# A hybrid backbone step: denser front, spread loads, early root and bias, context attention inside the Hyena stage

## What is computed

```
sh1,sc1,g1,sh2,sc2,g2 = silu(cond) @ w_mod + b_mod       # 1024 x 6144, two cond vectors
u   = layer_norm(x) * (1 + sc1) + sh1
q,k,v,xr,gate,hy = u @ w_in                              # 1024 x 2816
att = softmax(q k / 8 [+ rel. position bias]) v          # context: 128 x 128 keys, 8 heads of 64
                                                         # latent: window of the grid + 128 cached keys
rg  = bidirectional RG-LRU(xr) * gelu(gate)              # scans over tokens; has a sqrt
hyo = order-2 Hyena(hy)                                  # two long convolutions by Fourier tables
x   = layer_norm(ALPHA x + g1 * ([att,rg,hyo] @ w_out))
x   = layer_norm(ALPHA x + g2 * moe(layer_norm(x) * (1 + sc2) + sh2))   # top 2 of 16 experts
```

## Time and profile before

| | |
|---|---|
| median of runs | 751.33 us |
| profiled execution, whole | 748.11 us |
| its span | 746.3 us |
| busy, of the span | TensorE 90%, VectorE 62%, ScalarE 40%, GpSimd 18% |
| mean granted TensorE clock | 0.977 |
| DMA | 162.64 MB, mean 218 GB/s |

### The profile page before, as it was taken

How to read it: one execution, slowest core, us unless ns; L and a number is a source line. 1 busy time by engine, 2 the same in 40 slices (tenths; PEclk the granted TensorE clock), 3 DMA queues, 4 the chain that set the end, 5 groups by cost and what they waited for, 6 DMA issues and landing times. The chain is left out here.

```text
span 746.3 us, 9550 instructions
## 1 busy us (share of the span) xinstructions
PE 674.0 (90%) x3478; PEld 505.7 (68%) x3478; DVE 464.6 (62%) x762; ACT 295.3 (40%) x494; POOL 134.6 (18%) x111
## 2 busy tenths in 40 slices
PE   1898999999999778989899999889999999998990
PEld 0234999989999544568788898446777777766440
DVE  4536677809945446556434977866667777756268
ACT  2535423144444400176421110505665665654321
POOL 0002223345522032513200000011110011100230
PEclk9999999999999999999899999989999999999996
DMA  9752552224311778559807103626999999988362
GB/s 311 296 195 102 203 152 86 85 85 128 127 57 57 249 250 320 169 182 282 279 2 285 81 29 128 267 84 236 395 409 408 423 424 422 383 301 317 132 262 113
DMA packets 38448, 162.64 MB, mean 218 GB/s; under 512 B 4224, under 2 KB 13824, under 8 KB 25602
## 3 DMA queue, kind: packets, MB, share of 16 engines
q1 hardware_dynamic: 25488, 109.59, 40.7%
q10 hardware_dynamic: 7938, 34.22, 11.8%
q0 software_dynamic: 4976, 18.22, 6.4%
HBM read 140.23 MB, written 21.01 MB: 216 GB/s over the span
## 5 line engine op out<-in xcount | busy, mean ns | idle before, releaser
L2039 DVE TENSOR_TENSOR gate_up_low<-arena,gate_up_high 128x1024 fp32r<-128x1024 f32 x80 | 94.2, 1222 | 52.2 <-ACT gate_up_high L1011 49.5
L1011 ACT ACTIVATE gate_up_high<-arena 128x1024 fp32r<-128x1024 f32 x80 | 79.9, 1054 | 10.2 <-DMA arena<-in_moe_w_gu 10.1
L635 POOL TENSOR_TENSOR w_low<-arena,w_high 128x1024 fp32r<-128x1024 f32 x22 | 53.4, 2431 | 163.2 <-ACT w_high L754 163.2
L1450 PE MATMUL bank<-arena 128*128 128x256 f32 x320 | 70.3, 380 | 0.0
L1575 PE MATMUL bank<-arena 128*128 128x512 f32 x152 | 68.7, 594 | 1.0 <-ACT arena L1051 1.0
L1554 PE MATMUL bank<-gate_up_high,xt_high 128*128 128x512 f32 x152 | 61.8, 406 | 4.7 <-DVE xt_low L2125 4.7
L1450 PEld LDWEIGHTS bank<-arena 128*128 128x128 f32 x320 | 60.3, 190 | 8.0
L1554 PE MATMUL bank<-gate_up_low,xt_high 128*128 128x512 f32 x152 | 60.0, 395 | 0.0
L1554 PE MATMUL bank<-gate_up_high,xt_low 128*128 128x512 f32 x152 | 59.9, 394 | 0.0
L1285 PE MATMUL bank<-u_high,w_high 128*128 128x320 f32 x176 | 56.0, 318 | 3.4 <-DVE u_low L1749 3.3
L754 ACT ACTIVATE w_high<-arena 128x1024 fp32r<-128x1024 f32 x22 | 23.2, 1059 | 85.4 <-PE bank L1286 75.3
(11 more groups left out here) (318 smaller groups left out, 1298.8 us busy)
## 6 DMA issues: line engine op xcount, KB each, us to landing
arena<-in_moe_w_gu SPq DMA_DIRECT2D x40, 1024.0 KB, 8.8
arena<-in_w_mod SPq DMA_DIRECT2D x24, 1024.0 KB, 5.6
arena<-in_moe_w_down ACTq DMA_DIRECT2D x13, 1024.0 KB, 9.7
arena<-in_w_in SPq DMA_DIRECT2D x11, 1024.0 KB, 5.9
y_scr<-arena ACTq DMA_DIRECT2D x19, 512.0 KB, 6.3
arena<-in_moe_w_down SPq DMA_DIRECT2D x6, 1024.0 KB, 8.3
arena<-in_x SPq DMA_DIRECT2D x10, 512.0 KB, 7.7
y_scr<-arena SPq DMA_DIRECT2D x10, 512.0 KB, 7.0
```

What stands on the lines that cost most here:

```text
L635: G.tensor_tensor(WL[s_][:, :, w], ring[s_][:, :, w], WH[m % 2].bitcast(F), ALU.subtract).then_inc(wl_rdy, 1)
L1011: S.activation(WGH[j][c], raw_gu[s][:, c, :, :], ACT.Copy).then_inc(wgh_rdy, 1)
L1450: last = mm(B[2 * (i % 2) + q // 2][:, (q % 2) * 256:(q % 2 + 1) * 256], MT[:, k, i * P:(i + 1) * P], wo[q][:, k, :], start=(k == 0), stop ...
L2039: tt_(WGL[s][c], raw_gu[s][:, c, :, :], WGH[j][c].bitcast(F), ALU.subtract).then_inc(wgl_rdy, 1)
```

## The change

- `consts` holds `cond` first; `cond32[k]` is a 32-column slice that begins with the two cond columns of k. `mod_block` uses it as stationary and writes all 32 partitions of each group; only two are read.
- `filter_rows` takes a list of tiles. Tile pairs with different 64-row halves are issued alternately, into five bank pairs in place of one; the first pair stands ahead of `mod1(0)`; `spectrum` moves up, with other banks and waits.
- `front_dense`: nine filler matmuls before and between the filter layers, two more ahead of the projections.
- `rg_root(1)` moves to m = 20 of the projections.
- `rel_bias(0)`, `(1)` are issued behind `mod2_block(2)`, `(3)` once the recurrence is finished (`rg_fin`); GpSimd adds their masks behind the y tiles of o = 0; bias buffers move.
- The stores of `mod_scr` move from ScalarE's queue to SyncE's, ahead of the `VS` copies.
- `first_norm` is split: `first_gates` (1 MB) behind group 5, `first_norm` (1 MB) behind group 6, `gate_up_weights(0)` behind group 7.
- Attention steps 0 to 3 go. In their place, all heads at once in banks 2 and 1: `ctx_scores` in `forward(0)` behind ft = 0, `ctx_turned` between `mod2(3)` and `mod2(4)`, `ctx_values` in `inverse(0)` behind i = 0.

```diff
+        cond32 = [arena[:, 2 * k:2 * k + 32] for k in range(KT)]
-                    last = mm(mod_rows(bank, g), cond[:, k, :], w[:, 512 * g:512 * (g + 1)], ...)
+                    last = mm(bank[32 * g:32 * g + 32, :], cond32[k], w[:, 512 * g:512 * (g + 1)], ...)
...
+            front_dense(1)
             filter_layer(0)
+            front_dense(4)
             filter_layer(1)
             eng.wait_ge(modc_in, 1)
+            front_dense(4)
+            eng.wait_ge(filt_sin, 2)
+            eng.wait_ge(ld_tables, 48)
+            filter_rows([(0, 0), (1, 1)])
             mod1(0)
-            filter_rows(0)
+            eng.wait_ge(filt_read, 2)
+            filter_rows([(2, 1), (4, 0)])
             mod1(1)
-            filter_rows(1)
+            eng.wait_ge(eo_win, 2)
+            filter_rows([(3, 1)], 2)
             mod1(2)
-            filter_rows(2)
+            spectrum(0, 0)
             mod1(3)
-            spectrum(0, 0)
             spectrum(1, 0)
-            filter_rows(3)
+            spectrum(2, 0)
             mod1(4)
-            spectrum(2, 0)
             spectrum(3, 0)
-            filter_rows(4)
             mod1(5)
...
+                if m == 20:
+                    rg_root(1)
...
+            for b in range(2 * KT):
+                mod2_block(b)
+                if b == 2:
+                    eng.wait_ge(rg_fin, 1)
+                    rel_bias(0)
+                elif b == 3:
+                    rel_bias(1)
+            eng.wait_ge(mr_ev, 8)
+            for g in range(4):
+                eng.dma_start(mod_scr..., mrow2[g]...).then_inc(mr_st, 16)
...
+            def ctx_scores():
+                for hp in range(4):
+                    for j in range(2):
+                        r = slice(64 * j, 64 * j + 64)
+                        last = mm(B[2 - j][:, hp * P:(hp + 1) * P], QT[r, hp, 0:NCTX], KTt[r, hp, 0:NCTX], ...)
+                last.then_inc(s_mm, 4)
+            def ctx_turned():
+                for j in range(2):
+                    eng.wait_ge(p_rdy, 4 * (j + 1))
+                    for hp in range(4):
+                        last = T.transpose(B[2 - j][:, hp * P:(hp + 1) * P], PRc[:, 4 * j + hp, :], ident)
+                    last.then_inc(pt_mm, 4)
+            def ctx_values():
+                ...
+                for h in range(H):
+                    last = mm(B[2][:, hd], PTc[h % 2][...], VT[:, 0, hd], ...)
...
-            scores(0)
-            for p in range(19):
+            scores(4)
+            for p in range(4, 19):
```

More of the change, by code:

```diff
@@ L187, in build @@
         PTs = [h2.take(2, KW + P) for _ in range(2)]
+        h2.at = h1.end - 4 * 2 * NTOK
+        BM = [h2.take(4, KW + P) for _ in range(2)]
         assert h2.at <= AFTER1 + 4 * D
@@ L667, in _ @@
                     after(y_rdy)
[L669 to L674, removed]
+                if o == 0:
                     eng.wait_ge(rg_fin, 1)
-                    eng.dma_start(masks, t["masks"].rearrange("p (a b) -> p a b", a=3)).then_inc(mask_in, 16)
                     eng.wait_ge(mask_in, 16)
[L678 to L684, removed]
+                    bias(0)
+                    bias(1)
+            for g in range(2, 8):
+                bias(g)
             for i in range(TT):
@@ L957, in ot_copy @@
                     after(ot_ev)
-            for p in range(20 + 1):
+            for p in range(4, 20 + 1):
                 for j in range(2 if p < 20 else 0):
@@ L1246, in _ @@
             ut(1)
-            eng.wait_ge(spec_ev, 1)
             ut(2)
             eng.wait_ge(spec_ev, 4)
+            for b in range(2):
+                mm(B[2][:, :], ident, consts[:, 2 * KT:], start=True, stop=True)
             def hyt(c):
@@ L1357, in inverse @@
                     last.then_inc(inv_mm, 1)
+                    if o == 0 and i == 0:
+                        ctx_values()
                     if o == 0:
@@ L1940, in _ @@
                     after(z_ev)
+                    if o == 0 and ft == 0:
+                        eng.wait_ge(s_mm, 4)
+                        for j in range(2):
+                            V.tensor_reduce(soft[:, 0, 4 * j:4 * j + 4], B[2 - j][:, :].rearrange("p (a b) -> p a b", a=4),
+                                            AX.X, ALU.max, negate=True).then_inc(s_read, 4)
+                            after(s_read, 4)
                 for i in range(3):
@@ L1957, in _ @@
                     after(z_next)
+                    if o == 0 and i == 0:
+                        eng.wait_ge(pv_mm, 8)
+                        eng.wait_ge(p_rdy, 8)
+                        step(V.reciprocal(soft[:, 2, 0:8], soft[:, 1, 0:8]))
+                        for j in range(2):
+                            last = tt_(OS[0].rearrange("p (k j d) -> p k j d", k=4, j=2)[:, :, j, :],
+                                       B[2][:, :].rearrange("p (k j d) -> p k j d", k=4, j=2)[:, :, j, :],
+                                       soft[:, 2, 4 * j:4 * j + 4].unsqueeze(2).to_broadcast([P, 4, HD]), ALU.mult)
+                        last.then_inc(o_rdy, 1)
+                        after(o_rdy)
             mod2_rows(1)
-            for p in range(20 + 2):
+            for p in range(4, 20 + 2):
                 for j in range(2 if p < 20 else 0):
```

188 lines of the change are left out of this document (100 added, 88 removed).

## The result

The changed kernel takes 726.8 us where the kernel before, run beside it, takes 752.3: 25.5 us faster by the medians. Three of its four runs lie between 725.2 and 727.2 us; the fourth, at a mean granted clock of 0.62, took 1034.5 us and is left out of the ratio, which is 0.968, interval 0.963 to 0.973. The forecast was 29.6 us off, 721.7 us. The second set of runs of the same program gave 725.3 us (718.9 to 731.3), ratio 0.964 (0.957 to 0.971). The profiled executions stand at 748.1 and 726.3 us, so they show 21.8 of it; what follows goes by them.

A forecast was written before the change was run, and what follows sets the result against it. TensorE was taken as the bound, through half-clock work and waits. Gains 14.3 + 4.0 + 6.0 + 6.0 less 0.7 gave 29.6 us: 718.5 profiled, 721.7 with 3.2 added for the median; range 712 to 734.

The forecast's parts named there:

- signs of being wrong: Early blocks still at 1.89 us, `mod2` waiting over 3 us for DMA, or step 8 or 16 waiting for GpSimd.
- Front: Up to the modulation columns: fillers raise the clock early and pairing saves matmuls; done at 52.4, not 66.7, gain 14.3 us.
- rival A: Front clock stays low until the spectra or falls back in two waits: 5 of 14.3 us, total 731; chance 0.13.
- Wider blocks: Modulation with 32-column stationaries: 0.03 us more a block, 0.7 us lost over 24 blocks.
- Hyena: Hyena stage: earlier root and scans, no y-tile wait; last transposes at 307.5, not 311.5, gain 4.0 us after context work.
- `mod2(0)` at 250.0 as before: Start of the Hyena stage: its first block keeps its old time, with `forward(0)` and blocks ending `mod2(3)` at 263.3.
- Rival C: Hyena is bound by its blocks and context work comes on top: gain 0 instead of 4, total 726; chance 0.08.
- Start of attention: Hyena's transposes to step 8: context steps gone, bias group 2 next to be late; gain 5.3 to 6.7, taken as 6.0 us.
- Bias later: Attention from step 8: spread loads remove the late bias at step 16; gain 6.0 us, between 2 and 6.4.
- Rival B: Bias load and mask set the attention's pace: both attention gains fall from 12 to 6, total 728; chance 0.15.
- Rival D: 32-column matmuls no longer run side by side: 2.5 us more on 24 blocks, 60 us, total about 775; chance 0.04.

The follow-up runs named there:

- five things: The run of four things plus two idle matmuls ahead of step 10's transposes: 720.2 us, ratio 0.959.
- run of four things: Changed kernel without front fillers, two fillers ahead of the context keys, group 2's bias ahead of VS, attention loads spread anew: 719.4 us, ratio 0.959.

## Why the prediction was right or wrong

**The whole.** The median of 726.8 us is inside the range, 712 to 734, and just above the 717 to 726 that had the chance of 0.50 (the second set, 725.3, is just inside). In profiled executions I forecast 718.5 and 726.3 came: 7.8 us short, not 5.1. The difference is luck: I added 3.2 us because the profiled execution of before lay that far under its median, and that of the change lies only 0.5 under. So are the 1.9 us of the rest. The four stages together gave 10.5 us less than forecast. Of the signs of being wrong that I named, one came: step 8 waits for GpSimd.

**Front, 11.6 for 14.3: right mechanism, size off.** The level rose before the first block, as forecast, and pairs run side by side. Of the 2.7 missing, 1.6 come from the fall behind the wait for VectorE's second tile: block and spectrum took 4.6 us from 29.5 to 34.06, walked at 2.7 from 29.8 to 32.5. The wait itself (1.37) was forecast at 1.6; that the clock would not survive it was rival A, which came true for 3 us and not for the stage. The other 1.0 is in the sum: from 34.06 to the end of the last block (50.13) 16.1 us, walked at 15.1, since a row of two spectrum matmuls takes up to 1.92 from its start to the next group's, not 1.71. A further 0.2 are a slip: 47.7 and a tail of 4.9 make 52.6, not 52.4. And the fillers, to which I gave the rise, were not needed for it: the run without them is as good.

**Wider blocks, 0.7: right.** Blocks start 0.99 us before what follows, narrow ones 0.97; the run with narrow ones is equal. The Trainium skill (TensorE: Matmul & The Clock Gate, The mechanism) has weight loads pulled ahead of running matmuls where the row groups don't conflict or where the load goes to the background weight buffer. By the first alone the loads of 32 columns would show; here they lengthen a block by 0.02 us.

**Hyena, 2.7 for 4.0.** The scans end where they should (237.2; forecast "near 235"), and no y tile is waited for. The step that failed is "`mod2(0)` at 250.0 as before", with its price for a block at full clock. It began at the right moment (238.4 = 250.0 - 11.6) but at half clock: 5.4 us to the end of the context scores where the profiles with a fast first block have 4.0. These 1.4 us are the miss (58.8 us from the block to the transposes, the forecast had 57.5). Rival C, a gain of 0, did not hold, and the context work was priced right (4.1 us in the records, 3.3 of 3.6 felt when doubled). The waits for `mod2`'s weights came to 2.9 us (2.60 and 0.33), just within the 3 us I had allowed.

**Start of attention, 3.8 for 6.0.** TensorE's part is exact: step 4's transposes 8.4 us behind Hyena's, forecast 8.6. The load was mis-sized. I gave it 4.5 to 6.5 from issue to landing by the median of the earlier trace rows; it took 7.5, from 307.33 to 314.87, behind a 1 MB `w_out` piece issued 0.56 us before. The prediction counted the ten small issues ahead of it and forgot the large transfer. Issued ahead of that piece and of the copies, at 302.4, it lands in 4.8 us and step 8 is on time; which of the two held it more was not separated.

**Bias later, 1.7 for 6.0.** The spreading did its part: no wait over 0.34 us after step 8, and 6.32 come back without it. What failed is the silent premise that steps 9 to 15 run at 2.9 us. Behind the new wait they ran at half clock to 333: 18.4 us for four steps, 13.3 with the clock held. The prediction also names a rate here that its own times don't give: from 335.64 to 361.0 for eight steps is 3.2 us a step, not 3.3; nothing else rests on it. Rival B was half right at 0.15: load and mask were the next limit of this stage (9.6 us where 8.1 were to be had), and they stopped each improvement, at step 8, then 10, then 18. But the chain with an empty queue takes 7.2 us, so it is what is loaded beside it that makes it the limit.

**Rival D** is excluded: 32-column groups run side by side (1.06 us a block). Its price was added up wrong: 751.3 and 60 less 30 is 781, not 775.

## What to carry to other kernels

A wait taken out of a pipeline fed through two buffers came back a few steps on, as long as the feeding chain (here 4.8 us from first issue to landing with an empty queue, 6.5 to 10.6 with other loads beside it, and 2.4 for the mask) was not shorter than the steps it spans; write that chain out before pricing any wait. Price a load by what is queued ahead of it in bytes, not by the median landing of its kind. Where TensorE waits, count on half-clock work behind the wait: at step 8 that was 2 to 7 us beside a wait of 3.7. Four idle matmuls in the wait kept the clock up, but the next wait for a load took part of it back and the median did not move beyond the spread.

## What the runs showed of the hardware beyond that

Whether the clock falls behind a short wait differs between executions of the same instructions. Three places show it:

- At 238 us TensorE waits 1.5 us for ScalarE, then 0.78. The next block was slow in seven of the ten profiles with nothing idle ahead, at full clock in three; with a pair of idle matmuls before the context keys it was full in all three. Slow, it costs 1.4 to 1.6 us up to the end of the context scores.
- Behind the wait of 1.7 to 2.6 us for `mod2`'s weights, from 271 to 281, the work was slow in four of the thirteen profiles: in two of them in the block and the row behind it (1.85 and 4.59 us), in two in the row alone (5.42 for 3.73). These last two are the runs of four and of five things, whose first block was kept fast. So the full clock at 238 did not shorten their Hyena stage (58.7 and 58.1 us; the two other fast starts without added work 56.5).
- In the front, the wait of 1.37 to 1.40 us at 28 was followed by a slow block in eight of nine profiles; in the three without the nine front fillers (waits of 1.25 and 1.16 us, and none) in none. Counted from the first pair of tiles, the columns are done after 35.9 to 36.1 us with the slow block and after 34.4 to 34.6 in the four profiles with neither it nor idle matmuls in the wait.

What decides was not found.

Small loads fill the DMA engines at a lower rate: from 310 to 315 in the run of four things, with `VS` copies and group 3's bias, the DMA share was 1.02 at 259 GB/s, where large loads reached 413 at the same share.
